# Down projections of two MLPs: one 512-column product for the high and low activations

## The reference

```python
def _sq_relu_mlp(h, w_up, w_down):
    u = jax.nn.relu(h @ w_up)
    return (u * u) @ w_down
...
x = x + _sq_relu_mlp(_rmsnorm(x, a_norm_mlp[i]), a_w_up[i], a_w_down[i])
...
x = x + _sq_relu_mlp(_rmsnorm(x, b_norm_mlp[j]), b_w_up[j], b_w_down[j])
```

## Time and profile before

| | |
|---|---|
| median of 3 runs | 1176.01 us (1175.8 to 1176.9) |
| the profiled execution | 1175.98 us, of which the profiled span is 1174.2 us |
| TensorE products busy | 1154.3 us, 98% of the span, 9150 of them |
| VectorE, ScalarE, GpSimd busy | 893.1, 757.8 and 340.5 us |
| granted TensorE clock | 1.0 of full speed |
| from HBM | 211 MB, 181 GB/s over the span |

### The profile page before, as it was taken

The page is one execution under the profiler, slowest core; times in us unless marked ns, Lnnn a source line. Parts: engine busy times, 40 slices in busy tenths (PEclk is TensorE's granted clock), DMA queues, the critical chain, the costliest instruction groups (busy, mean ns, idle before and its releaser), DMA issues.

```text
span 1174.2 us, 26850 instructions
## 1 busy us (share of the span) xinstructions
PE 1154.3 (98%) x9150; PEld 1086.4 (93%) x9150; DVE 893.1 (76%) x1491; ACT 757.8 (65%) x1373; POOL 340.5 (29%) x303
## 2 busy tenths in 40 slices
PE   9999999999999999999999999999999999999998
PEld 8888999999998999999998779999889978999987
DVE  7788777666578877756659979999556776899964
ACT  7766655444565755554557878888556666988852
POOL 3320355300012245522302205555000310455500
PEclk9999999999999999999999999999999999999999
DMA  9554566655655466665654445666745643566673
GB/s 327 176 156 140 178 197 197 197 188 192 215 157 161 147 197 197 198 214 187 203 183 132 139 143 182 197 197 202 228 159 170 241 148 126 187 201 197 202 218 105
DMA packets 64056, 216.64 MB, mean 185 GB/s; under 512 B 7777, under 2 KB 10993, under 8 KB 63985
## 3 DMA queue, kind: packets, MB, share of 16 engines
q1 hardware_dynamic: 63808, 215.17, 56.7%
q10 hardware_dynamic: 176, 0.54, 0.2%
HBM read 211.47 MB, written 1.06 MB: 181 GB/s over the span
## 4 chain that ended last, share of the span: by engine, by line
PE 82%; DVE 10%; ACT 3%; issue 2%; POOL 1%; DMA 1%; SPq 0%; DVEq 0%; POOLq 0%; ACTq 0%
PE bank L785 16%; PE bank L786 16%; PE bank L787 16%; PE bank L712 4%; PE bank L714 4%; PE bank L713 4%; PE bank L661 3%; DVE w_lo L1601 3%; PE bank L663 3%; PE bank L662 3%; PE bank L590 2%; PE bank L591 2%; PE bank L596 1%; PE bank L915 1%; PE bank L932 1%
## 5 line engine op out<-in xcount | busy, mean ns | idle before, releaser
L1601 DVE TENSOR_TENSOR w_lo<-raw,w_hi 128x1024 fp32r<-128x1024 f32 x386 | 505.5, 1318 | 75.1 <-ACT w_hi L1139 73.8
L1139 ACT CAST w_hi<-raw 128x1024 fp32r<-128x1024 f32 x386 | 402.1, 1046 | 239.5 <-PE bank L787 100.9
L785 PE MATMUL bank<-h_hi,w_hi 128*128 128x256 f32 x1184 | 326.9, 276 | 0.4
L786 PE MATMUL bank<-h_lo,w_hi 128*128 128x256 f32 x1184 | 325.6, 275 | 0.0
L787 PE MATMUL bank<-h_hi,w_lo 128*128 128x256 f32 x1184 | 325.6, 275 | 0.0
L785 PEld LDWEIGHTS bank<-h_hi,w_hi 128*128 128x128 f32 x1184 | 227.3, 192 | 1.4 <-DVE h_lo L1675 1.2
L786 PEld LDWEIGHTS bank<-h_lo,w_hi 128*128 128x128 f32 x1184 | 227.3, 192 | 0.1
L787 PEld LDWEIGHTS bank<-h_hi,w_lo 128*128 128x128 f32 x1184 | 227.3, 192 | 0.0
L785 PE MATMUL bank<-a_hi,w_hi 128*128 128x256 f32 x544 | 150.1, 276 | 1.2 <-DVE a_lo L1675 1.1
L786 PE MATMUL bank<-a_lo,w_hi 128*128 128x256 f32 x544 | 149.6, 275 | 0.0
L787 PE MATMUL bank<-a_hi,w_lo 128*128 128x256 f32 x544 | 149.6, 275 | 0.0
(11 more groups left out here) (222 smaller groups left out, 2107.7 us busy)
## 6 DMA issues: line engine op xcount, KB each, us to landing
raw<-in_w_up_sb SPq DMA_DIRECT2D x44, 512.0 KB, 3.4
raw<-in_w_up_fox SPq DMA_DIRECT2D x44, 512.0 KB, 3.5
raw<-in_w_up_a SPq DMA_DIRECT2D x32, 512.0 KB, 3.5
raw<-in_w_down_a SPq DMA_DIRECT2D x32, 512.0 KB, 4.6
raw<-in_w_up_b SPq DMA_DIRECT2D x32, 512.0 KB, 3.4
raw<-in_w_down_b SPq DMA_DIRECT2D x32, 512.0 KB, 4.7
raw<-in_w_in_sb SPq DMA_DIRECT2D x24, 512.0 KB, 3.7
raw<-in_w_in_fox SPq DMA_DIRECT2D x24, 512.0 KB, 3.5
```

What stands on the lines that cost most here:

```text
L785: nc.tensor.matmul(dst, w_hi[:, slot, w], in_turns(src_hi[:, at + k, :]), start=begin, stop=False)
L786: nc.tensor.matmul(dst, w_hi[:, slot, w], in_turns(src_lo[:, at + k, :]), start=False, stop=False)
L1139: nc.scalar.copy(w_hi[:, slot, 0:k * P], raw[:, slot, 0:k * P]).then_inc(hi_ready, 1)
L1601: nc.vector.tensor_tensor(w_lo[:, slot, 0:k * P], raw[:, slot, 0:k * P], w_hi[:, slot, 0:k * P].bitcast(f32), ALU.subtract).then_inc(lo_re ...
```

## The change

`a_hi` and `a_lo` become the two halves of one tensor `a`, and in `down_a` and `down_b` (`WIDE`) each k-tile has two products in place of three: w_hi with both halves as a moving operand of 512 columns, which fills the whole bank (the product with the high part in columns 0 to 255, that with the low part in 256 to 511), and w_lo with the high half, 256 columns, into the first half of the bank. Within a k-tile w_lo's product stands first, but in the tile's first k-tile the wide one does. VectorE adds first one half of the bank to `X`, waits for that add on a new semaphore, `high_added`, then adds the other half. `tile_out` is counted by the second add.

```diff
--- before.py
+++ after.py
@@ -187,11 +187,11 @@
             def mlp_sb(name, shape, dt=f32):
                 return mlp.enter_context(nc.sbuf_tensor(name, shape, dt))
 
-            a_hi = mlp_sb("a_hi", [P, D_FF // P, TOK], f32r)
-            a_lo = mlp_sb("a_lo", [P, D_FF // P, TOK], f32r)
+            a = mlp_sb("a", [P, 2, D_FF // P, TOK], f32r)
             c_buf2 = mlp_sb("conv_buf", [P, 4, TOK])
             prod = mlp_sb("prod", [P, 2, TOK])
 
+        a_hi, a_lo = a[:, 0], a[:, 1]
         x_tok = ZM[:].rearrange("p k t -> p (k t)").rearrange("p (a f) -> p a f", a=2)
         y_tok = H[:].rearrange("p k t -> p (k t)").rearrange("p (a f) -> p a f", a=2)
         g_tok = X[:].rearrange("p k t -> p (k t)").rearrange("p (a f) -> p a f", a=2)
@@ -300,6 +300,7 @@
         gain_in = sem("gain_in")
         gain_squared = sem("gain_squared")
         gain_joined = sem("gain_joined")
+        high_added = sem("high_added")
         y_half = sem("y_half")
         y_squared = sem("y_squared")
         y_first_ready = sem("y_first_ready")
@@ -357,6 +358,7 @@
         PRODUCTS = {"up_a": 0, "up_b": D_FF // P, "up_sb": 2 * D_FF // P, "up_fox": 2 * D_FF // P + D_FF2 // P}
         DOWN_OF = {"down_a": "up_a", "down_b": "up_b"}
         FIRST_TAP = {"up_sb": 0, "up_fox": 2 * D_FF2 // P}
+        WIDE = {"down_a": 0, "down_b": D // P}
         OUT_BANK = (0, 1, 4, 5)
         FIRST = slice(0, KT * P // 2)
         SQUARED = {name: {(0, 0): 1, (1, 0): 2 if name.startswith("out") else 3,
@@ -393,6 +395,14 @@
         def product(b):
 
             return bank[b][:, 0:TOK].rearrange("p (a h) -> p h a", h=2)
+
+        def high_and_low(x, k):
+
+            return x[:, :, k, :].rearrange("p s (h a) -> p s a h", h=2)
+
+        def low_product(b):
+
+            return bank[b][:, TOK:2 * TOK].rearrange("p (a h) -> p h a", h=2)
 
         def geometry(u):
 
@@ -782,6 +792,15 @@
                                 pe.wait_ge(*operand_tile(k))
                             if first and s == 0:
                                 pe.wait_ge(h_lo, operand_count(name, 0, 0, k))
+                            if name in WIDE:
+                                both, pair = bank[b][:], high_and_low(a, at + k)
+                                if begin:
+                                    nc.tensor.matmul(both, w_hi[:, slot, w], pair, start=True, stop=False)
+                                last = nc.tensor.matmul(dst, w_lo[:, slot, w], in_turns(src_hi[:, at + k, :]),
+                                                        start=False, stop=False)
+                                if not begin:
+                                    last = nc.tensor.matmul(both, w_hi[:, slot, w], pair, start=False, stop=end)
+                                continue
                             nc.tensor.matmul(dst, w_hi[:, slot, w], in_turns(src_hi[:, at + k, :]), start=begin, stop=False)
                             nc.tensor.matmul(dst, w_hi[:, slot, w], in_turns(src_lo[:, at + k, :]), start=False, stop=False)
                             last = nc.tensor.matmul(dst, w_lo[:, slot, w], in_turns(src_hi[:, at + k, :]), start=False,
@@ -1683,7 +1702,9 @@
                 def tile(i, done, b, first):
                     dve.wait_ge(units_done, done)
                     x = halves_of(X[:, i * per + b, :])
-                    nc.vector.tensor_tensor(x, product(b), x, ALU.add).then_inc(tile_out, 1)
+                    nc.vector.tensor_tensor(x, product(b), x, ALU.add).then_inc(high_added, 1)
+                    dve.wait_ge(high_added, i * per + (WIDE[name] + b + 1))
+                    nc.vector.tensor_tensor(x, low_product(b), x, ALU.add).then_inc(tile_out, 1)
                     for operand, hi, lo in operands:
                         low(operand, X, hi, lo, i, per, b)
                     if behind is not None and (i, b) == behind[:2]:
```

## The result

The changed kernel takes 1178.42 us, the median of 15 runs (1177.6 to 1179.3), against 1176.14 for 15 runs of the kernel before on the same chip. The ratio is 1.0019, with a 95% interval from 1.0012 to 1.0025. So the change costs 2.3 us where 2.9 us less was forecast. It lies outside the forecast's range, on the other side, and just inside the 2.35 us that the prediction had called no change. The profiled execution took 1178.21 us, with a span of 1176.4, which is 2.2 us more than before's 1174.2.

What follows compares the result with a forecast made beforehand. TensorE's stream of products, filling 98% of the span, was taken as the bound. Products save 3.84 us and stage ends cost 0.92, so 1175.98 - 2.92 gives 1173.1 us, with an 8 in 10 range of 1171.1 to 1175.9.

Steps and rivals of the forecast that it cites:

- The wide pair saves 7.50 ns, 3.84 us in all: TensorE in `down_a` and `down_b`: one 512-column product at 215.83 ns replaces two costing 223.33, over 512 k-tiles.
- The narrow product stays at 111.67 ns: TensorE, both down stages: the 256-column w_lo product keeps its pace, since the next w_hi loads beside it.
- the rival in which it speeds up: Narrow product runs at 107.9 ns beside a wide one: 1.9 us more saved, 1171.2 us; chance 0.09.
- the rival in which a wide product costs what two narrow ones do: The array takes 512 columns as two passes, so only the stage ends count: 1176.9 us; chance 0.11.
- a saving of 1.3 us in all: Saving on the product pairs by the skill's N / 2.4 + 2.5 ns formula: only 2.5 ns a pair.
- The second piece is free: The wide product's operand lies in both halves of `a`; the forecast charged nothing for reading two pieces.
- The rival on the slower side, through the wide product's read: Jumping between halves upsets the stream 512 times; slower from 10.3 ns a product, up to 1225.8 us; chance 0.08.
- The second add comes 0.46 us behind the first, and that is paid at both stage ends: VectorE delays `tile_out` by 0.46 us; TensorE stands still at the ends of `down_a` and `down_b`: 0.92 us more.
- No stall in mid-stage: Inside a down stage the weight split has 1.1 us to spare; about 0.5 us stays, so TensorE doesn't wait.
- The sum: Whole kernel: 3.84 us saved on products less 0.92 at stage ends gives 2.92 us less, 1173.1 us; chance 0.58.
- The last sentence of the prediction: Signs of being wrong: a mid-stage split wait, wide starts over 216 ns apart, or time changed outside both stages and ends.

Runs made afterwards that it cites:

- e2_apart: The changed kernel, but `up_sb`, `down_sb`, `up_fox` and `down_fox` use two separate tensors in the same memory as the halves of `a`; 1173.31 us, ratio 0.9976.
- e1_layout: The kernel before with only `a_hi` and `a_lo` laid out as halves of one tensor, no wide product or second add; 1180.06 us, ratio 1.0033.
- e5_shifted: e2_apart with `g_lo` used from its third row on, so its offset differs from that of `g_hi` by 512 elements; 1177.91 us, ratio 1.0015.

## Why the prediction was wrong

The forecast was 2.92 us less; 2.3 us more was measured.

- *The wide pair saves 7.50 ns, 3.84 us in all.* Right. Both stages took 83.84 us, 1.92 less each.
- *The narrow product stays at 111.67 ns.* Right: 0.11 us from its start to the next. 83.84 us for 256 k-tiles is 327.5 ns each, and that rules out the rival in which it speeds up and the rival in which a wide product costs what two narrow ones do. It rules out a saving of 1.3 us in all as well.
- *The second piece is free.* Right, by the same number. The rival on the slower side, through the wide product's read, didn't happen.
- *The second add comes 0.46 us behind the first, and that is paid at both stage ends.* Right in the trace: 0.46 us between the adds and not 0.34, and 0.44 and 0.46 us at the two ends. Without the add the ends take 0.90 us less, and covering it gains 1.1 us with the restart.
- *No stall in mid-stage.* Right: the stages' lengths leave no room for one.
- *The sum.* Right for what it counted: e2_apart is 2.92 us faster than before. That it agrees to the hundredth is luck, since its interval is 1.8 to 3.9 us.
- *The step that failed* is the first edit of the diff, `a_hi` and `a_lo` as halves of `a`. The part on the change goes from TensorE to VectorE's second add and gives this edit no line and no price, which is to cost it at nothing everywhere. What the runs show in its place is 4.94 us in the changed kernel (2.31 and 2.63), 3.8 us by itself in e1_layout, and 4.5 us through a second address in e5_shifted: VectorE's low part comes later and loses to GpSimd, and TensorE waits for the split behind it. The last sentence of the prediction, on time lost outside the two stages, names the sign that came, but no rival stood for it, and 0.08 was all that the slower side had, on another mechanism.

The trace of before held what was needed. The two names are also written in `up_sb` and `up_fox`, at line 1711, which the prediction never looked up. There VectorE was busy for 85.04 of 88.00 us (727 to 815), not the 51 of 85.76 in `down_a`, and it led GpSimd by 0.04 us in each pair. With that, a rival would have read: the low part needs a second address, starts later and loses up to 22 races in each stage; VectorE's 10.64 us for a period grows past TensorE's 10.72. The price of a lost race, 0.43 us, stands only in the later traces, and with it the size is somewhere between nothing and 22 x 0.43 x 2 = 19 us; but the sign would have been on the table.

In `up_b` line 1732 has its second address too, and it costs nothing there: between the values of `in_b` and `down_b` the account has only the stage end's 0.44 us. `up_a` lies ahead of `down_a`'s start, in the 0.22 us that I put down to the start of the program.

## What to carry to other kernels

Follow every name that an edit touches to all its users, also where only its layout changes: operands that shared one computed offset may need two, here 13 to 53 ns on the engine's queue. That was nothing in `up_b`, and over 2 us in a stage in which VectorE's period was 99% of TensorE's and its instructions met GpSimd's. So find the stages in which the second engine has next to nothing to spare, look at its period against that of the bound, and ask of every edit what it does there. When an edit's stages come out as forecast and the total doesn't, a table of how far ahead the kernel is at the same instruction finds the place at once.
